# Expert outputs scaled at eviction and added to the output row by row, instead of stored, gathered and summed at the end

## The reference, cut to what matters

```python
def hierarchical_moe(h, w_group, b_group, w_er, b_er, w_gate, w_up, w_down):
    ...                                   # top-1 group, then top-2 experts within it
    top_p = jax.nn.softmax(top_v, axis=-1) * g_w
    expert_id = g_sel[:, None] * EXPERTS_PER_GROUP + top_i
    comb = jnp.sum(jax.nn.one_hot(expert_id, N_EXPERTS, dtype=jnp.float32) * top_p[..., None], axis=1)
    hg = jnp.einsum('td,edf->tef', t, w_gate)
    hu = jnp.einsum('td,edf->tef', t, w_up)
    act = jax.nn.silu(hg) * hu * comb[..., None].astype(hg.dtype)
    out = jnp.einsum('tef,efd->td', act, w_down)
...
    h = h + hierarchical_moe(n2, ...)     # n2 = rms_norm(h, norm2_g)
```

## Time and profile before

| | |
|---|---|
| median of 3 runs | 1687.53 us |
| profiled execution: its own time, its span | 1688.26 us, 1686.4 us |
| busy in the span: PE, DVE, ACT, POOL | 89%, 61%, 42%, 35% |
| granted TensorE clock, mean | 0.947 |
| chain that ended last, by engine | PE 77%, DVE 10%, issue 5%, ACT 4%, DMA 2% |
| DMA | 196.69 MB, mean 117 GB/s |

### The profile page before, as it was taken

One profiled execution on the slowest core, in us unless ns is written; L12 is line 12 of the kernel. 1 busy time (PEld: TensorE's weight loads), 2 busy tenths in 40 slices (PEclk: granted clock), 3 DMA queues, 4 the chain that ended last, 5 costly groups with the idle time before them and its releaser, 6 DMA issues.

```text
span 1686.4 us, 19621 instructions
## 1 busy us (share of the span) xinstructions
PE 1507.3 (89%) x7262; PEld 1233.9 (73%) x7262; DVE 1020.4 (61%) x1466; ACT 701.2 (42%) x1144; POOL 590.8 (35%) x398
## 2 busy tenths in 40 slices
PE   6989999998998979999999999999973888899970
PEld 5877898876987755776888788888833777777760
DVE  3249999999995767662000033363046888888864
ACT  5247112534234356663222232232233666666640
POOL 2310223344223251000222223322123877777634
PEclk9989999999999979999999999999985999999995
DMA  5200121131210122102112134434056877857468
GB/s 182 62 19 1 46 49 38 32 113 42 71 38 26 63 75 76 51 13 69 44 51 62 63 131 150 143 125 156 28 200 224 299 249 242 307 175 248 164 229 307
DMA packets 83501, 196.69 MB, mean 117 GB/s; under 512 B 10574, under 2 KB 32334, under 8 KB 81102
## 3 DMA queue, kind: packets, MB, share of 16 engines
q1 hardware_dynamic: 68430, 146.67, 26.8%
q0 software_dynamic: 11232, 40.90, 6.9%
q10 hardware_dynamic: 3744, 7.87, 1.2%
HBM read 198.55 MB, written 40.89 MB: 142 GB/s over the span
## 4 chain that ended last, share of the span: by engine, by line
PE 77%; DVE 10%; issue 5%; ACT 4%; DMA 2%; POOL 1%; ACTq 0%; SPq 0%; DVEq 0%; POOLq 0%
PE ps L643 22%; PE ps L644 21%; PE ps L645 21%; PE ps L842 3%; DVE dist L1351 2%; DVE e_lo L1618 2%; PE ps L832 2%; PE ps L898 2%; DMA t_y<-y_dram,slot 1%; ACT e_hi L1253 1%; PE ps L859 1%; ACT junk L1073 1%; DMA xin<-in_x 1%; PE ps L784 1%; PE ps L771 1%
## 5 line engine op out<-in xcount | busy, mean ns | idle before, releaser
L1690 POOL TENSOR_TENSOR w_lo<-w_raw,w_hi 128x512 fp32r<-128x512 f32 (+1 forms) x160 | 216.9, 1358 | 696.9 <-ACT w_hi L963 696.3
L963 ACT CAST w_hi<-w_raw 128x512 fp32r<-128x512 f32 (+1 forms) x160 | 97.5, 615 | 499.8 <-PE ps L645 465.2
L643 PE MATMUL ps<-w_hi,n_hi 128*128 128x512 f32 (+2 forms) x704 | 244.9, 348 | 8.8 <-POOL w_lo L1690 6.8
L645 PE MATMUL ps<-w_hi,n_lo 128*128 128x512 f32 (+2 forms) x704 | 242.8, 345 | 0.0
L644 PE MATMUL ps<-w_lo,n_hi 128*128 128x512 f32 (+2 forms) x704 | 242.8, 345 | 0.0
L1464 DVE TENSOR_TENSOR a_lo<-a_raw,a_hi 128x1024 fp32r<-128x1024 f32 x32 | 40.0, 1254 | 292.4 <-ACT a_hi L1204 292.2
L1253 ACT CAST e_hi<-e_raw 128x2048 fp32r<-128x2048 f32 x93 | 174.7, 1913 | 84.6 <-PE ps L645 68.7
L1618 DVE TENSOR_TENSOR e_lo<-e_raw,e_hi 128x2048 fp32r<-128x2048 f32 x62 | 194.2, 3134 | 22.9 <-ACT e_hi L1253 22.1
L1831 POOL TENSOR_TENSOR e_lo<-e_raw,e_hi 128x2048 fp32r<-128x2048 f32 x31 | 166.8, 5381 | 73.9 <-ACT e_hi L1253 73.2
L1388 DVE MAX8 small<-dist 128x8 f32<-128x384 f32 (+5 forms) x192 | 171.8, 895 | 6.6
L643 PE MATMUL ps<-n_hi,w_hi 128*128 128x512 f32 x448 | 175.5, 392 | 0.0
(11 more groups left out here) (246 smaller groups left out, 2833.6 us busy)
## 6 DMA issues: line engine op xcount, KB each, us to landing
e_raw<-in_w_gate SPq DMA_DIRECT2D x62, 512.0 KB
e_raw<-in_w_up SPq DMA_DIRECT2D x62, 512.0 KB
e_raw<-in_w_down SPq DMA_DIRECT2D x31, 1024.0 KB
w_raw<-in_w_in SPq DMA_DIRECT2D x72, 256.0 KB, 2.7
y_dram<-e_y POOLq DMA_DIRECT2D x31, 512.0 KB, 5.4
a_raw<-att_dram SPq DMA_DIRECT2D x16, 512.0 KB, 3.4
a_raw<-ret_dram SPq DMA_DIRECT2D x16, 512.0 KB, 3.5
w_raw<-in_w_in SPq DMA_DIRECT2D x40, 128.0 KB, 2.4
```

The lines of the kernel that those rows point to most:

```text
L643: mm(out, a[0], b[0], start=first, stop=False, skip_group_check=skip)
L645: return mm(out, a[1], b[0], start=False, stop=last, skip_group_check=skip)
L963: nc.scalar.copy(w_hi[c % NH][:, :width], w_raw[c % NR][:, :width]).then_inc(hi_ready, 1)
L1690: G.tensor_tensor(w_lo[c % NH][:, :width], w_raw[c % NR][:, :width], w_hi[c % NH][:, :width].bitcast(F32), ALU.subtract).then_inc(lo_ready, 1)
```

## The change

Each expert tile's rows are multiplied by the weight of their slot when they are evicted, and GpSimd adds them straight to `out` with one indirect DMA per tile.

- SP stores `h` to `out` in place of `h_dram`, and `out` has 128 more rows, for the padding slots, which one more store fills. Nothing is loaded again, and the whole end is gone.
- The token numbers are made from 1 up, so that 0 marks a padding slot: `token` is the number less 1 (at least 0), and a second list `dest` is the row to add to: the token, or for a padding slot one of the 128 extra rows, a different one for each partition. GpSimd's gathers now wait for `dest` too.
- The weight of each slot comes from a second product of the same kind: `tile_p` (high and low part of p1 and p2) times `hot`, 16 matmuls of 64 columns (`slot_weights`), which TensorE does after the first tile's transposes and VectorE adds up into `p_slot`.
- `rows_out` multiplies by the column of `p_slot` instead of copying.
- `add_rows(i)` takes the place of `store_y(i)`. A token's two rows may lie in different tiles, so an add waits until the one before has landed.

```diff
-    c[:, K_TOK:K_TOK + 2 * NT] = np.tile(np.arange(NT) * float(P), 2)[None, :] + p
+    c[:, K_TOK:K_TOK + 2 * NT] = np.tile(np.arange(NT) * float(P), 2)[None, :] + p + 1
@@ SP
-                sp.dma_start(h_dram[t * P:(t + 1) * P, :], h_sb[:, t, :]).then_inc(h_stored, 16)
+                sp.dma_start(out[t * P:(t + 1) * P, :], h_sb[:, t, :]).then_inc(h_stored, 16)
+                if t == 0:
+                    sp.dma_start(out[S:S + P, :], h_sb[:, t, :]).then_inc(h_stored, 16)
...
-            for t in range(NT):
-                if t == 6:
-                    sp.wait_ge(exT_full, NTILE)
-                sp.dma_start(t_h[t][:], h_dram[t * P:(t + 1) * P, :]).then_inc(th_in, 16)
-            for t in range(NT):
-                sp.wait_ge(t_sum, t + 1)
-                sp.dma_start(out[t * P:(t + 1) * P, :], t_h[t][:]).then_inc(t_out, 16)
-            sp.wait_ge(t_out, 16 * NT)
+            for i in range(2):
+                sp.wait_ge(ey_out[i], 16 * ((NTILE + 1 - i) // 2))
@@ TensorE
+            def slot_weights():
+                name = ("p_slot",)
+                pe.wait_ge(p_done2, 1)
+                pe.wait_ge(ranked, 1)
+                for n in range(2 * NT):
+                    last = mm(bank(name, 64), hot[:, n, :], tile_p[:, n].rearrange("p a i -> p (a i)"),
+                              start=n == 0, stop=n == 2 * NT - 1)
+                bk.filled(last, name)
...
             turn_rows(Step(0))
+            slot_weights()
@@ VectorE
-            V.tensor_copy(token[:], bank(("token",), 32)).then_inc(token_done, 1)
+            V.tensor_scalar(token[:], bank(("token",), 32), -1.0, 0.0, ALU.add, ALU.max).then_inc(token_done, 1)
+            bk.read(V.tensor_copy(small[:, 384:416], bank(("token",), 32)), ("token",))
+            bk.wait_read(dve, ("token",))
+            seq(V.tensor_scalar(small[:, 464:496], small[:, 384:416], 0.0, pad_row[:], ALU.is_equal, ALU.mult))
+            V.scalar_tensor_tensor(dest[:], small[:, 464:496], -1.0, small[:, 384:416], ALU.add, ALU.add).then_inc(dest_done, 1)
...
+            both = small[:, 304:320]
+            seq(V.tensor_copy(p_hi[:], both))
+            seq(V.tensor_tensor(p_lo[:], both, p_hi[:].bitcast(F32), ALU.subtract))
...
+            seq(V.memset(spot, 0.0))
+            seq(V.tensor_tensor(spot[:, :, 0:31], at_least[:, :, 0:31], at_least[:, :, 1:32], ALU.subtract))
+            for j, part in enumerate((p_hi, p_lo)):
+                inst = V.tensor_tensor(tile_p[:, :, j, :], spot, part[:].bitcast(F32).unsqueeze(2).to_broadcast([P, NS, 32]), ALU.mult)
+            inst.then_inc(p_done2, 1)
+
+            def slot_weights():
+                name = ("p_slot",)
+                bk.wait_full(dve, name)
+                seq(V.tensor_copy(p_slot, bank(name, 32)))
+                seq(V.tensor_tensor(p_slot, p_slot, bank(name, 64)[:, 32:], ALU.add))
...
-                V.tensor_copy(e_y[i.parity][:], ps[:, B_Y:B_Y + D]).then_inc(ey_read, 1)
+                n = tile_at(i)
+                V.tensor_scalar(e_y[i.parity][:], ps[:, B_Y:B_Y + D], p_slot[:, n:n + 1], None, ALU.mult).then_inc(ey_read, 1)
...
-            for t in range(NT):
-                dve.wait_ge(ty_in[t % 3], 32 * (t // 3 + 1))
-                y0, y1 = (y[:] for y in t_y[t % 3])
-                V.scalar_tensor_tensor(t_h[t][:], y0, small[:, 304 + t:305 + t], t_h[t][:], ALU.mult, ALU.add).then_inc(t_half, 1)
-                dve.wait_ge(t_half, t + 1)
-                V.scalar_tensor_tensor(t_h[t][:], y1, small[:, 312 + t:313 + t], t_h[t][:], ALU.mult, ALU.add).then_inc(t_sum, 1)
@@ GpSimd
-            def store_y(i):
+            def add_rows(i):
                 pool.wait_ge(ey_read, i.n + 1)
-                pool.dma_start(y_dram[tile_at(i) * P:(tile_at(i) + 1) * P, :], e_y[i.parity][:]).then_inc(ey_out[i.parity], 16)
+                if i.reached(1):
+                    pool.wait_ge(ey_out[(i - 1).parity], 16 * ((i - 1).half + 1))
+                n = tile_at(i)
+                G.indirect_dma_start(out=out, out_offset=bass.IndirectOffsetOnAxis(ap=dest[:, n:n + 1], axis=0),
+                                     in_=e_y[i.parity][:], in_offset=None, compute_op=ALU.add).then_inc(ey_out[i.parity], 16)
...
             pool.wait_ge(token_done, 1)
+            pool.wait_ge(dest_done, 1)
...
-            for t in range(NT):
-                if t >= 3:
-                    pool.wait_ge(t_sum, t - 2)
-                for j in range(2):
-                    G.indirect_dma_start(out=t_y[t % 3][j][:], out_offset=None, in_=y_dram,
-                                         in_offset=bass.IndirectOffsetOnAxis(ap=slot[:, j, t:t + 1], axis=0)).then_inc(ty_in[t % 3], 16)
```

More of the change, by code:

```diff
@@ L221, in program @@
         token = sb("token", [P, 32], U32)
+        dest = sb("dest", [P, 32], U32)
+        pad_row = sb("pad_row", [P, 1])
+        p_slot = small[:, 432:464]
         nt_at = place[0]
@@ L308, in program @@
         tile_tok = sb("tile_tok", [P, 2 * NT, 32], F32R, at=dist_at + 4 * 4 * NT * NE)
+        tile_p = sb("tile_p", [P, 2 * NT, 2, 32], F32R, at=r1 + 4 * 17760)
+        p_hi = sb("p_hi", [P, 2 * NT], F32R, at=r1 + 4 * 18784)
+        p_lo = sb("p_lo", [P, 2 * NT], F32R, at=r1 + 4 * 18800)
         hot = sb("hot", [P, 2 * NT, P], F32R, at=dist_at + 4 * (16 * NT * NE + (NT + 1) * NE))
@@ L324, in program @@
         at_lo = sb("at_lo", [P, 2, P], F32R, at=e_at + 16 * D + 12 * FF)
-        t_h = [sb(f"t_h{t}", [P, D], at=nt_at + 4 * W3 + t * 4 * D) if t < 6 else r1t(f"t_h{t}", [P, D], 15424 + (t - 6) * D)
-               for t in range(NT)]
-        t_y = [[sb(f"t_y{i}{j}", [P, D], at=nt_at + (2 * i + j) * 4 * D) for j in range(2)] for i in range(3)]
         ident = cst[:, K_ID:K_ID + P]
@@ L335, in program @@
         S_QR = 432
-        q_dram, att_dram, ret_dram, h_dram = scratch["q"], scratch["att"], scratch["ret"], scratch["h"]
-        n2_dram, y_dram = scratch["n2"], scratch["y"]
+        q_dram, att_dram, ret_dram = scratch["q"], scratch["att"], scratch["ret"]
+        n2_dram = scratch["n2"]
         const_in, up_in = sem("const_in"), sem("up_in")
@@ L380, in program @@
         ey_full, ey_read, ey_out = sem("ey_full"), sem("ey_read"), [sem(f"ey_out{i}") for i in range(2)]
-        ty_in, th_in = [sem(f"ty_in{i}") for i in range(3)], sem("th_in")
-        t_half, t_sum, t_out = sem("t_half"), sem("t_sum"), sem("t_out")
+        dest_done, p_done2 = sem("dest_done"), sem("p_done2")
         def cols(src, c0, n, at=0):
@@ L501, in program @@
         bk.use(("token",), 7)
+        bk.use(("p_slot",), 6)
         B_XT, B_GU, B_AT, B_Y = 0, 2 * BANK, 3 * BANK, 4 * BANK
@@ L621, in _ @@
             each_step(load_expert, NTILE - 1)
-            sp.wait_ge(h_stored, 16 * NT)
-            for j in range(3):
-                sp.wait_ge(elo_done[j], NTILE - 1)
-            for t in range(NT):
-                if t == 6:
-                    sp.wait_ge(exT_full, NTILE)
-                sp.dma_start(t_h[t][:], h_dram[t * P:(t + 1) * P, :]).then_inc(th_in, 16)
-            for t in range(NT):
-                sp.wait_ge(t_sum, t + 1)
-                sp.dma_start(out[t * P:(t + 1) * P, :], t_h[t][:]).then_inc(t_out, 16)
-            sp.wait_ge(t_out, 16 * NT)
+            for i in range(2):
+                sp.wait_ge(ey_out[i], 16 * ((NTILE + 1 - i) // 2))
         @block.tensor
@@ L1262, in _ @@
             act.wait_ge(n2_stored, 16 * NT)
-            act.wait_ge(h_stored, 16 * NT)
+            act.wait_ge(h_stored, 16 * (NT + 1))
             x_part(Step(0))
@@ L1515, in _ @@
             seq(V.memset(ones[:], 1.0))
+            seq(V.tensor_scalar(pad_row[:], cst[:, K_REL:K_REL + 1], -1.0, float(S + 1), ALU.mult, ALU.add))
             name = ("lgt",)
@@ L1633, in rows_out @@
                     dve.wait_ge(ey_out[i.parity], 16 * i.half)
[L1634 removed]
+                n = tile_at(i)
+                V.tensor_scalar(e_y[i.parity][:], ps[:, B_Y:B_Y + D], p_slot[:, n:n + 1], None, ALU.mult).then_inc(ey_read, 1)
             dve.wait_ge(n2_stored, 16 * NT)
[L1636 removed]
+            dve.wait_ge(h_stored, 16 * (NT + 1))
             w_part(Step(0), 0)
@@ L1822, in _ @@
             pool.wait_ge(token_done, 1)
+            pool.wait_ge(dest_done, 1)
             pool.wait_ge(n2_stored, 16 * NT)
-            pool.wait_ge(h_stored, 16 * NT)
+            pool.wait_ge(h_stored, 16 * (NT + 1))
             for i in range(NX):
@@ L1834, in work @@
                 if i.reached(2):
-                    store_y(i - 2)
+                    add_rows(i - 2)
             each_step(work, NTILE)
-            store_y(Step(NTILE - 1))
+            add_rows(Step(NTILE - 1))
             for i in range(2):
@@ L1876 @@
         w[name[3:]] = nc.dram_tensor(name, a.shape, F32, kind="ExternalInput").ap()
-    out = nc.dram_tensor("out", (S, D), F32, kind="ExternalOutput").ap()
-    scratch = {n: nc.dram_tensor(f"{n}_dram", (S, D), F32, kind=SCRATCH).ap() for n in ("q", "att", "ret", "h", "n2")}
```

(5 more changed lines are left out.)

2 lines of the change are left out of this document (1 added, 1 removed).

## The result

The changed kernel takes 1660.5 us (median of 4 runs, 1659.0 to 1662.8) against 1687.6 (1687.4 to 1687.9): ratio 0.984, 95% interval 0.9823 to 0.9857. That is faster by 27 us, where 47 were forecast. 1660.5 lies in the stated range, but above the 1629 to 1652 of its likeliest case.

What follows compares the result with a forecast made beforehand. Bound: TensorE's expert loop, stalled by VectorE and GpSimd excluding each other, then a 45.2 us sequential tail. 1688.3 - 33.3 (tail) + 1.8 (ahead) - 15.6 (loop) = 1641.2, median 1640.5; range 1630 to 1685.

Steps and rivals of the forecast that it cites:

- likeliest case: Whole kernel: tail, start and loop terms all come as worked out, 1629 to 1652 us; chance 0.58.
- the two rivals: Whole kernel: the long step stays (chance 0.16), or adds set the pace but stay faster (0.13); range up to 1685.
- L: An add's time from issue to landing: taken as 7.5 us, bounds 3.3 and 12.7.
- The tail: After the last eviction: gathers, sums, loads and stores go, the last two adds in series replace them; -33.3 us.
- Ahead of the loop: +1.8: Before the loop: small VectorE instructions and 16 weight matmuls start tile 1 at 1298.2 instead of 1296.37.
- the order at the port: Loop: VectorE's e_lo goes before GpSimd's; long 14.7 us steps go, all 10.3, -25.8; one long step returns late, +4.4.
- The term of +5.8: Loop, dense weight loads: the adds' extra reads cost 5.8 us, as late weights or adds landing after 10.3.
- an issue of up to 2.7 us costs nothing: Loop, GpSimd: the add has room from T + 0.87 to T + 3.6, T being the end of VectorE's L1618.
- is free for L below 10.3: Loop: waiting for the add before costs nothing, since adds are issued 10.3 us apart.
- The long step stays: Rival, loop: order at the port does not change, the loop keeps its time, 1656 us; chance 0.16.
- The adds set the pace: Rival, loop: landings between 10.3 and 11.7 us, 31 in series; with 11, median 1665; chance 0.13.
- Slower: Rival: the chain of adds outlasts loop and tail, landings above 11.7 us; with 13, median 1727; chance 0.13.

Runs made afterwards that it cites:

- e2: Changed kernel with the add made a plain indirect write to the same rows, wait for the one before kept; 1640.1 us, ratio 0.9725.
- e9: Changed kernel with the experts' weights loaded only for the first two steps; 1640.4 us, ratio 0.9731.
- e4: Kernel before with its direct store of e_y issued as an indirect DMA to the same rows, no wait added; 1668.4 us, ratio 0.9901.
- e12: Kernel before with one added wait: GpSimd's e_lo begins only after VectorE's e_lo row of the same tile, in every step; 1673.7 us, ratio 0.9925.
- e3: Changed kernel with the add replaced by the direct store to an array of its own, no wait for the one before; 1651.9 us, ratio 0.9797.
- e1: Changed kernel with each add waiting only for the add two steps before, so two are in flight; 1639.0 us, ratio 0.9723.
- e6: e1 with the add issued ahead of the gather in each step instead of behind it; 1663.2 us, ratio 0.985.
- e7: e1 without GpSimd's final landing wait, and GpSimd's e_lo waiting for VectorE's in the last three steps; 1633.3 us, ratio 0.967.
- e8: Changed kernel without GpSimd's final landing wait, and GpSimd's e_lo waiting for VectorE's in the last three steps; 1654.4 us, ratio 0.9794.
- e5: Changed kernel without GpSimd's own wait for the last landings at its program's end (SyncE still waits); 1657.4 us, ratio 0.9816.

## Why the prediction was right or wrong

**As a whole.** The sign was right, and the range held, but by its upper part, which was there for the two rivals; 20 of the 47 us forecast did not come: 15.3 of them are the loop's and 4.8 the tail's. The sign named for a wrong forecast, an L under load above 10.3, was met: the landings of the loop took up to 12.4.

**The tail: the sequence right, its end missed.** The last add was to land at 1653.1 and landed at 1653.4. That is luck. L was taken at 7.5 and measured 6.14, twice 1.4 less; but the last but one add was issued at 1640.34, not 1638.06, since it waited for the one before (2.3 more), and the last one 0.75 behind the landing. What failed is the step "End: 1638.06 + 2 x 7.5 = 1653.1": the program does not end with the landing. GpSimd's drain of 5.13 was in no term, because in the trace of before it lies hidden, and I read only busy rows. Saved: 28.5 instead of 33.3.

The estimate by the Trainium skill (Collectives: The Full Stack, "Why ReduceScatter is half of AllGather") was 6.7 against 6.14 measured, nearer than my 7.5, but its two parts missed in opposite ways: a plain indirect write lands after 3.32 (e2, the last row of this document) and not after 5.19, and the sum adds 2.8 and not 1.5. Its reason can be looked at in the packets: those of q0 take 8.5% of 1658.9 here and 5.4% of 1640.1 in e2, where only the sum is missing:

```profile
q0 software_dynamic: 8928, 32.51, 5.4%
```

That is (141.0 - 88.6) / 31 = 1.7 us of all engines more for each add, on top of 88.6 / 62 = 1.4 for a plain transfer: about double, which agrees with the page's two reads for one. It does not prove them, for packet time is no fixed price: the same 62 transfers took more in e9, where no weights ran beside them (158.8 us):

```profile
q0 software_dynamic: 8928, 32.51, 9.7%
```

**Ahead of the loop: +1.8, measured +1.8 at the transposes, +2.5 at the first eviction.** `token` was 1.2 earlier in this execution, so it is read against that: tile 1's transposes started 9.63 behind it before (1296.37 - 1286.74) and 11.40 now (1296.91 - 1285.51). The first eviction went from 28.5 to 31.0 behind `token`. In the other kernels with these edits it is 30.1 to 31.2, and in e4 and e12, which lack them, 29.1 and 29.4, so part of the 2.5 is scatter. The way there is as worked out: the 16 matmuls take 3.60, from 1293.49, and tile 1 follows them.

**The loop, the order at the port: right.** That the long step goes, that each step then takes 10.3, and that it comes back once where no gather is left (14.8), all stood as forecast, and e3, e4 and e12 show its cause. Without late adds the loop is 306.0 (e1): 20.0 less, where -25.8 + 4.4 = -21.4 were worked out.

**The loop, what comes back: the step that failed.** The term of +5.8, for late weights or late adds, measured 19.7 (325.7 - 306.0). It was hardly worked out: four tiles of 0.52 MB at 338 GB/s are 6.2, and that is the time of the bytes and not of a wait. Two claims behind it were wrong. That "an issue of up to 2.7 us costs nothing" holds only when it begins ahead of VectorE's `w_part(0)`, with 0.23 us of margin; behind it the whole issue is added to the step (e1, e6, e2). And that the added wait "is free for L below 10.3" overlooks the 0.8 us between a landing that is waited for and the issue: by these rows an add in its usual place may take 10.5 - 0.8 = 9.7, an estimate, and one that was itself kept back less; the 9.33 above was already late. I put the issue at 0.94 from the gathers; with the sum it is 1.55 to 1.6, so each slip costs 1.6. That part is a size; the mechanism that turned it into step time was not in the forecast. "Late weights", the other half of the term, did not come: the adds' bytes made no weights late (e1 moves the same ones). The late adds did come, by the load of the weights (e9).

**The rivals.** "The long step stays" comes near the time (1656 against 1660.5) for the wrong reason: the loop kept its length, but not its long steps. "The adds set the pace": its test, adds that wait for the one before, was met in 15 of 31 and not in each step, and the loop's time is not 31 landings in series but steps of 10.3 and 11.9. "Slower" did not come: a few landings were longer than 11.7, but 15 of the 30 adds behind the first did not stand waiting for one.

**The best version.** e7, 1633.3 (ratio 0.967), 27 below the changed kernel. It rests on a property of the routing: a token's two experts are of one group, and steps i and i-1 work on tiles h and 16+h, so two adds in flight touch no common row only while no group of experts spans both tiles. These inputs meet that. A group that spans both must have 16 tiles; four of them may be nearly empty, one for each of its experts, so it takes about three quarters of all rows in one group (1540 of 2048). Such a routing was not tried. For any routing e8 is the best measured, 1654.4.

## What to carry to other kernels

Work that is moved onto a shared port is priced by where it begins relative to the other engine's instruction, not only by how long it is: ask by how many tenths of a microsecond it keeps its place, and what could push it out. A serial chain of read-add-write transfers must be priced with its landing time under load (here up to twice that of the quiet tail) plus the delay behind its wait, and two in flight did as much here as transfers of half the landing time (e1 and e2, 1639.0 and 1640.1). When a change makes another engine's instruction the last of the program, look for what that engine does at the end, though it is not counted as busy.

## What the runs showed of the hardware

- An indirect DMA that adds takes 1.55 us to issue on GpSimd, the same one without the sum 0.96, and in the quiet tail it lands after 6.14 in place of 3.32 (the row of e2's chain below).
- GpSimd's drain at the end takes 5.13 us when all has landed; begun before the last add's landing (e5), it ends 2.6 us behind it.
- An add that had to wait for a landing was issued 0.75 to 0.80 us after it; one that did not, 0.30 us behind the gather before it.
- An add whose issue begins 0.23 us before VectorE's `e_lo` row runs beside it in 1.59 us; one that begins 0.35 us behind it takes 3.37, to 1.44 us after the row's end.
- Adds of 512 KB land after a median of 6.7 us with no weights beside them (e9), and after 9.3 to 12.4 us where the changed kernel waited for them in the loop.
- Who goes first at the port changed with 0.4 us: a third instruction of 0.99 in place of 0.59 (e4). An explicit wait fixes the order for 0.3 us a step (10.6 against 10.3), and e12 gains 13.5 us by that one line.

```profile
1626.49 3.32 DMA out<-e_y,dest
```
